# Accumulator halves over three PSUM banks, first and last two units by token half

## The reference, cut to what matters

```python
h = rms_norm(x, norm_mix_pre)
proj = h @ w_in                                  # 2048 -> 15664 columns
a_qkv, b_q, b_kv, b_gate, c_q, c_k, c_v, m_gate = jnp.split(proj, IN_OFFSETS, axis=-1)
o_a = dilated_attention(...)                     # 3 groups x 8 heads, windows 128, 512, 2048
o_b = nsa_attention(...)                         # 16 heads: compressed, selected, window branches
o_c = diff_attention(...)                        # 8 heads, two softmax maps each
g = sigmoid(m_gate.reshape(bsz, seq, 3, 2048))
mixed = g[:, :, 0] * (o_a @ w_branch_a) + g[:, :, 1] * (o_b @ w_branch_b) + g[:, :, 2] * (o_c @ w_branch_c)
x = x + rms_norm(mixed @ w_out, norm_mix_post)
x = x + rms_norm(square(relu(rms_norm(x, norm_mlp_pre) @ w_up)) @ w_down, norm_mlp_post)
```

## Time and profile before

| | |
|---|---|
| median of 3 runs | 1770.3 us (1768.73 to 1770.68) |
| the profiled execution | 1770.19 us |
| its span, first to last instruction | 1768.9 us |
| mean granted TensorE clock | 0.996 |
| TensorE busy | 1722.0 us (97%) |
| VectorE busy | 951.5 us (54%) |
| ScalarE busy | 841.3 us (48%) |
| DMA | 336.77 MB, 190 GB/s |

### The profile page before, as it was taken

One profiled execution on the slowest core, in us unless ns is written; L12 is line 12 of the kernel. 1 busy time (PEld: TensorE's weight loads), 2 busy tenths in 40 slices (PEclk: granted clock), 3 DMA queues, 4 the chain that ended last, 5 costly groups with the idle time before them and its releaser, 6 DMA issues.

```text
span 1768.9 us, 23930 instructions
## 1 busy us (share of the span) xinstructions
PE 1722.0 (97%) x8155; PEld 1401.1 (79%) x8155; DVE 951.5 (54%) x1338; ACT 841.3 (48%) x1269; POOL 55.2 (3%) x103
## 2 busy tenths in 40 slices
PE   7999999999999989999999989999999999999998
PEld 6888877777777878787888768888888888888886
DVE  5544455755555544465665465555444455554555
ACT  5443445655555555344444455444443344444442
POOL 1000010000000001000000000000000000000000
PEclk9999999999999999999999999999999999999999
DMA  7666665655566767846876565665556666655553
GB/s 236 204 181 183 194 171 133 171 154 158 164 167 191 183 176 225 277 144 220 291 239 225 190 181 176 190 182 186 190 192 194 195 189 183 188 183 185 193 195 136
DMA packets 168278, 336.77 MB, mean 190 GB/s; under 512 B 11408, under 2 KB 13664, under 8 KB 167680
## 3 DMA queue, kind: packets, MB, share of 16 engines
q1 hardware_dynamic: 162512, 317.17, 58.3%
q0 software_dynamic: 5552, 18.44, 4.5%
q10 hardware_dynamic: 128, 0.03, 0.0%
HBM read 327.11 MB, written 8.49 MB: 190 GB/s over the span
## 4 chain that ended last, share of the span: by engine, by line
PE 57%; DVE 2%; DMA 1%; ACT 1%; issue 1%; SPq 0%; ACTq 0%; DVEq 0%
PE ps L507 18%; PE ps L509 18%; PE ps L508 18%; PE ps L553 1%; DVE w_lo L1325 1%; DMA raw<-in_w_in_dram 1%; DMA gate_dram<-stage 0%; ACT w_hi L933 0%; DVE mid L1975 0%; PE ps L538 0%; PE ps L536 0%; PE ps L537 0%; DVE h_lo L1851 0%; PE ps L723 0%; PE ps L755 0%
## 5 line engine op out<-in xcount | busy, mean ns | idle before, releaser
L1325 DVE TENSOR_TENSOR w_lo<-raw,w_hi 128x1024 fp32r<-128x1024 f32 x576 | 703.2, 1225 | 685.7 <-ACT w_hi L933 666.1
L933 ACT ACTIVATE w_hi<-raw 128x1024 fp32r<-128x1024 f32 x576 | 607.2, 1059 | 636.1 <-PE ps L509 614.5
L507 PE MATMUL ps<-w_hi,h_hi 128*128 128x512 f32 (+1 forms) x1600 | 635.1, 397 | 21.7 <-ACT stage L1062 11.5
L509 PE MATMUL ps<-w_hi,h_lo 128*128 128x512 f32 (+1 forms) x1600 | 623.7, 390 | 0.0
L508 PE MATMUL ps<-w_lo,h_hi 128*128 128x512 f32 (+1 forms) x1600 | 623.0, 389 | 0.0
L507 PEld LDWEIGHTS ps<-w_hi,h_hi 128*128 128x128 f32 x1600 | 302.0, 189 | 104.2 <-issue 29.9
L509 PEld LDWEIGHTS ps<-w_hi,h_lo 128*128 128x128 f32 x1600 | 301.9, 189 | 63.5
L508 PEld LDWEIGHTS ps<-w_lo,h_hi 128*128 128x128 f32 x1600 | 302.5, 189 | 58.7
L507 PE MATMUL ps<-w_hi,u_hi 128*128 128x512 f32 x496 | 193.4, 390 | 0.0
L508 PE MATMUL ps<-w_lo,u_hi 128*128 128x512 f32 x496 | 193.0, 389 | 0.0
L509 PE MATMUL ps<-w_hi,u_lo 128*128 128x512 f32 x496 | 193.0, 389 | 0.0
(11 more groups left out here) (270 smaller groups left out, 925.8 us busy)
## 6 DMA issues: line engine op xcount, KB each, us to landing
raw<-in_w_in_dram SPq DMA_DIRECT2D x240, 512.0 KB, 3.7
raw<-in_w_up_dram SPq DMA_DIRECT2D x128, 512.0 KB, 3.8
raw<-in_w_down_dram SPq DMA_DIRECT2D x128, 512.0 KB, 4.3
raw<-in_w_out_dram SPq DMA_DIRECT2D x32, 512.0 KB, 4.2
bias<-bias_table POOLq DMA_DIRECT2D x72, 128.0 KB, 3.5
raw<-in_w_branch_b_dram SPq DMA_DIRECT2D x16, 512.0 KB, 5.5
raw<-in_w_branch_c_dram SPq DMA_DIRECT2D x16, 512.0 KB, 5.1
gate_dram<-stage SPq DMA_DIRECT2D x12, 512.0 KB, 5.8
```

The source lines that it names most:

```text
L507: pe.matmul(acc, hi[:, kc + k, tok], w_hi[:, slot, k, 0:cols], start=a, stop=False)
L509: mm = pe.matmul(acc, lo[:, kc + k, tok], w_hi[:, slot, k, 0:cols], start=False, stop=b)
L933: act.activation(w_hi[:, slot, :, :], raw[:, slot, :, :], ACT.Copy).then_inc(sem("hi_ready"), 1)
L1325: dve.tensor_tensor(w_lo[:, slot, :, :], raw[:, slot, :, :], w_hi[:, slot, :, :].bitcast(F32), ALU.subtract).then_inc(sem("lo_ready"), 1)
```

## The change

The two halves of chunk c of the slots go to banks by `slot_bank(c, t)`: banks 0, 1 and 6 in turn, (2c + t) mod 3. Bank 7 alone takes the outputs of all pairs (O_BANK), the C outputs are transposed into banks 7 and 5 (C_BANKS), the compressed probabilities into banks 4 and 5. TensorE's order in a chunk changes: in slot s = 0 it does half 0 of units 0 and 1 and half 1 of unit 0, in slot s = 1 half 1 of unit 1; the same in s = 6 and 7; between them each unit has half 0 and half 1 as before. Each half waits for `lo_ready` itself. The first half of a chunk waits for the evacuation of the second half of the chunk two before, the second half for the first half of the chunk before. The late transposes of slot 33 stand in slot 34, those of the C outputs in slots 152 to 155 instead of 152, 153, 155 and 157, and two of their splits two slots or one earlier.

```diff
...
 O_SLOT = {pr.o: p for p, pr in enumerate(PAIRS)}
 EXP_SLOT = {(pr.s + 2 if pr.kind == "a" else pr.s): p for p, pr in enumerate(PAIRS)}
 SCALE_SLOT = {(pr.s + 5 if pr.kind == "a" else pr.s + 1): p for p, pr in enumerate(PAIRS)}
-STAGE_T = {12: 6, 21: 7, 30: 8, 33: 9, 42: 10, 49: 11, 57: 12, 66: 13}
+STAGE_T = {12: 6, 21: 7, 30: 8, 34: 9, 42: 10, 49: 11, 57: 12, 66: 13}
 STAGE_CHUNK = {6: 0, 7: 1, 10: 4, 11: 5, 12: 6, 13: 7}
 BLOCKS_AT = [92, 93, 97, 98, 102, 103, 107, 108]
 B0 = 150
-C_AT = [2, 3, 5, 7]
-SPLIT_AT = [2, 2, 3, 4, 6, 8, 16, 16, 17, 17]
+C_AT = [2, 3, 4, 5]
+C_BANKS = [7, 5]
+SPLIT_AT = [2, 2, 3, 4, 5, 6, 16, 16, 17, 17]
+SLOT_BANKS = [0, 1, 6]
+O_BANK = 7
+def slot_bank(c, t):
+    return SLOT_BANKS[(2 * c + t) % 3]
 def stage_steps(n):
...
         values("v_a", 0, [tiles_out(Pos(T0["v_a"] - 1), 1, "v_a", 0)])
         with pe.Fori(1, 3) as i:
             values("v_a", i)
-        def slot_free(c):
-
-            if c <= 10:
-                return [[("evac_v", V0["q_b"] + c)], [("evac_s", S0["q_b"] + c)]]
-            return [[("evac_s", S0["gate"] + 2 * (c - 10) - 1 + t)] for t in range(2)]
+        def taken(c, t):
+            if c < 10:
+                return ("evac_s", S0["q_b"] + c + 1) if t else ("evac_v", V0["q_b"] + c + 1)
+            return "evac_s", S0["gate"] + 2 * (c - 10) + 1 + t
+        def slot_half(n, t):
+            c, s = divmod(n, CH)
+            cols = B_LAST if c == 3 else W
+            pe.wait_ge(sem("lo_ready"), XS + n + 1)
+            if s == 0:
+                if c == 0:
+                    pe.wait_ge(sem(("evac_v", "evac_s")[t]), (V0, S0)[t]["q_b"])
+                elif t:
+                    name, value = taken(c - 1, 0)
+                    pe.wait_ge(sem(name), value)
+                elif c == 1:
+                    pe.wait_ge(sem("tevac_v"), 6)
+                    pe.wait_ge(sem("tevac_s"), 6)
+                else:
+                    name, value = taken(c - 2, 1)
+                    pe.wait_ge(sem(name), value)
+            acc, tok, slot = ps[:, slot_bank(c, t), 0:cols], slice(t * P, (t + 1) * P), n % RING
+            for k in range(UR):
+                kc = UR * s + k
+                pe.matmul(acc, h_hi[:, kc, tok], w_hi[:, slot, k, 0:cols], start=kc == 0, stop=False)
+                pe.matmul(acc, h_hi[:, kc, tok], w_lo[:, slot, k, 0:cols], start=False, stop=False)
+                mm = pe.matmul(acc, h_lo[:, kc, tok], w_hi[:, slot, k, 0:cols], start=False, stop=kc == KC - 1)
+            if t:
+                mm.then_inc(sem("unit_used"), 1)
+            elif s == CH - 1:
+                mm.then_inc(sem("half_done"), 1)
         def late_tiles(n):
...
         def outputs(p):
             pr = PAIRS[p]
-            bank = 6 + pr.out % 2
+            bank = O_BANK
             pe.wait_ge(sem("pt_copied1"), p + 1)
             if pr.first:
-                wait(pe, sem("o_taken"), pr.out - 1)
+                wait(pe, sem("o_taken"), pr.out)
             if pr.kind == "c":
                 pt = p_t[:, 2 * (p % 2) + 1, :]
                 pe.matmul(ps[:, bank, 0:P], pt[:, 0:P], value(p, 0, 0), start=True, stop=True)
...
             pe.wait_ge(sem("compressed"), 1)
-            pe.wait_ge(sem("pt_copied1"), NPAIR)
+            pe.wait_ge(sem("o_split_lo"), 6)
             for t in range(2):
                 for h in range(8):
                     mm = pe.matmul(ps[:, 4 + t, 2 * NCMP * h:2 * NCMP * (h + 1)], q_b[:, h, t * P:(t + 1) * P],
...
             pe.wait_ge(sem("o_split_lo"), 6)
             for n in range(8):
                 q, t = n // 2, n % 2
-                tr = pe.transpose(ps[:, 6 + n // 4, P * (n % 4):P * (n % 4) + P],
+                tr = pe.transpose(ps[:, 4 + n // 4, P * (n % 4):P * (n % 4) + P],
                                   cmp_p[:, t, 4 * q:4 * q + 4, :].rearrange("p a n -> p (a n)"), ident[:, :])
             tr.then_inc(sem("cmp_pt"), 1)
...
         def output_transposes(j):
             pe.wait_ge(sem("c_ready"), 1)
+            pe.wait_ge(sem("pt_copied1"), NPAIR)
             pe.wait_ge(sem("o_taken"), 20)
             wait(pe, sem("o_split_lo"), j + 1 if j >= 2 else 0)
             for c in range(2):
                 for t in range(2):
-                    tr = pe.transpose(ps[:, 6 + j % 2, 256 * c + P * t:256 * c + P * t + P],
+                    tr = pe.transpose(ps[:, C_BANKS[j % 2], 256 * c + P * t:256 * c + P * t + P],
                                       o_c[:, t, P * (2 * j + c):P * (2 * j + c + 1)], ident[:, :])
             tr.then_inc(sem("o_transposed"), 1)
...
         for j, n in enumerate(C_AT):
             pe_steps.setdefault(n, []).append(lambda j=j: output_transposes(j))
         for n in range(NSLOT):
-            c, s = divmod(n, CH)
-            unit(Pos(XS + n), s % RING, h_hi, h_lo, UR * s, 0, B_LAST if c == 3 else W, s == 0, s == CH - 1,
-                 slot_free(c) if s == 0 else None)
+            s = n % CH
+            if s in (0, CH - 2):
+                slot_half(n, 0)
+                slot_half(n + 1, 0)
+            elif s not in (1, CH - 1):
+                slot_half(n, 0)
+            slot_half(n, 1)
             if n in STAGE_T:
                 late_tiles(n)
             if n in T_SLOT:
...
             if c >= 8:
                 act.wait_ge(sem("pv_done"), NA)
             dst = v_c[:, 1, W * (c - 8):W * (c - 7)] if c >= 8 else stage[:, c % 2, 1, 0:cols]
-            act.activation(dst, ps[:, 1, 0:cols], ACT.Copy, scale=scale).then_inc(sem("evac_s"), 1)
+            act.activation(dst, ps[:, slot_bank(c, 1), 0:cols], ACT.Copy, scale=scale).then_inc(sem("evac_s"), 1)
         def late_out(n):
...
                 wait(act, sem("gates_stored"), 16 * c)
             else:
                 act.wait_ge(sem("unit_used"), U0["gate"] + CH * (c + 1))
-            act.activation(stage[:, 0, h, :], ps[:, h, :], ACT.Tanh, scale=rstd_half[:, h:h + 1]).then_inc(
+            act.activation(stage[:, 0, h, :], ps[:, slot_bank(c + 10, h), :], ACT.Tanh, scale=rstd_half[:, h:h + 1]).then_inc(
                 sem("evac_s"), 1)
         def pt_copy(p):
...
             pr = PAIRS[p]
             act.wait_ge(sem("pv_done"), p + 1)
-            src = ps[:, 6 + pr.out % 2, 0:256]
+            src = ps[:, O_BANK, 0:256]
             if pr.kind == "a":
                 act.wait_ge(sem("table_stored"), 16)
                 act.activation(o_at[:, pr.out, :], src, ACT.Copy).then_inc(sem("o_taken"), 1)
...
                 act.wait_ge(sem("o_taken"), pr.out)
                 for t in range(2):
-                    sq = act.activation(c_square[:, t, :], ps[:, 6 + pr.out % 2, P * t:P * t + P], ACT.Square,
+                    sq = act.activation(c_square[:, t, :], ps[:, O_BANK, P * t:P * t + P], ACT.Square,
                                         accum_out=c_ssq[:, t, h:h + 1])
                 sq.then_inc(sem("o_taken"), 1)
...
                 act.wait_ge(sem("o_transposed"), q - 1)
                 act.wait_ge(sem("hidden_rows"), 2)
                 act.wait_ge(sem("const_loaded"), 16 * 6)
-                act.activation(o_hi[:, 8 + 2 * q:10 + 2 * q, :], ps[:, 6 + q % 2, :].rearrange("p (a n) -> p a n", a=2),
+                act.activation(o_hi[:, 8 + 2 * q:10 + 2 * q, :], ps[:, C_BANKS[q % 2], :].rearrange("p (a n) -> p a n", a=2),
                                ACT.Copy, scale=c_gain[:, 0:1]).then_inc(sem("o_split_hi"), 1)
             else:
                 act.wait_ge(sem("b_ready"), q - 5)
...
             if c >= 8:
                 dve.wait_ge(sem("pv_done"), NA)
             dst = v_c[:, 0, W * (c - 8):W * (c - 7)] if c >= 8 else stage[:, c % 2, 0, 0:cols]
-            dve.tensor_scalar(dst, ps[:, 0, 0:cols], scale, None, ALU.mult).then_inc(sem("evac_v"), 1)
+            dve.tensor_scalar(dst, ps[:, slot_bank(c, 0), 0:cols], scale, None, ALU.mult).then_inc(sem("evac_v"), 1)
         def late_out(n):
...
         def cmp_third():
             dve.wait_ge(sem("cmp_pt"), 1)
-            dve.tensor_copy(cmp_pt[:, :, :].rearrange("p (b a) n -> p b (a n)", b=2), ps[:, 6:8, :]).then_inc(
+            dve.tensor_copy(cmp_pt[:, :, :].rearrange("p (b a) n -> p b (a n)", b=2), ps[:, 4:6, :]).then_inc(
                 sem("cmp_pt_copied"), 1)
         def cmp_fourth(js):
...
                                   o_hi[:, 2 * q:2 * q + 2, :].bitcast(F32), ALU.subtract).then_inc(sem("o_split_lo"), 1)
             elif q < 6:
                 dve.scalar_tensor_tensor(o_lo[:, 8 + 2 * q:10 + 2 * q, :],
-                                         ps[:, 6 + q % 2, :].rearrange("p (a n) -> p a n", a=2), c_gain[:, 0:1],
+                                         ps[:, C_BANKS[q % 2], :].rearrange("p (a n) -> p a n", a=2), c_gain[:, 0:1],
                                          o_hi[:, 8 + 2 * q:10 + 2 * q, :].bitcast(F32), ALU.mult, ALU.subtract
                                          ).then_inc(sem("o_split_lo"), 1)
             else:
```

## The result

The changed kernel takes 1747.85 us, median of 4 runs (1746.88 to 1749.53), against 1769.66 us beside it (4 runs, 1768.73 to 1770.68): a ratio of 0.9873, 95% interval 0.9858 to 0.9887. It is faster by 21.8 us; 1749.0 were predicted. The profiled span is 1746.9 us against 1768.9.

What follows compares the result with a forecast made beforehand. TensorE, busy 1722.0 of 1768.9 us, bounds the kernel; only its idle time and low clock can be won. 21.0 + 1.0 + 2.3 - 1.0 - 2.0 = 21.3 us off 1770.3 gives 1749.0 us, range 1744 to 1753 (chance 0.70).

Steps and rivals of the forecast that it cites:

- Term one: Chunk starts in the slots: all 12 waits for tanh or evacuation go, 18.1 us plus 0.24 each, 21.0 us won.
- Term two: Doubled keys' late transposes, moved one unit later: their 1.0 us wait for VectorE's copies goes, 1.0 us won.
- Term three: Low clock after the waits near 247.5 and 573 us: 2.3 of 3.3 us lost counted as won.
- the clock at slot 142: Behind the grown w_lo wait of 1.9 us: a third of a 1.6 us clock loss counted.
- The tight places: Slot 118 and w_lo of 99, with its like in gate chunks: w_lo late, 1.0 us lost, bounds 0 and 3.
- at nothing: Single output bank, earlier C transposes (upper bound 1 us), single gate stage buffer and wait before the branches: no cost.
- Slot 142: Late raw weights: w_lo of 143 waited for 1.4 us more; 2.0 us lost with the clock, bounds 1.4 and 4.
- Rival 1: Gate chunks: ScalarE's first tanh is late and half the gates' waits come back; 1756.4 us, chance 0.12.
- rival 2: Starvation at 44 places with s = 0 and 6, w_lo wanted sooner; 1809 at full cost, chance 0.03.
- rival 4: Chunk starts: banks are not the limit, late w_lo would end each wait anyway; no change, 1770, chance 0.03.
- rival 5: Tight places grow to their bounds; 1754 us, chance 0.10.
- Rival 3: Clock falls at each of 22 chunk borders, 1.6 us lost each; 1784 us, chance 0.02.

Runs made afterwards that it cites:

- e3: Against the kernel before: two banks and the old order, the rest of the change kept (single output bank, moved transposes, w_lo waits per half); 1769.79 us, ratio 0.9996.
- e1: Whole change with three banks in rotation, but every unit in the old order (half 0, then half 1); 1747.59 us, ratio 0.9871 to the kernel before.
- e10: Whole change, but the doubled keys' transposes stay at slot 33; 1749.62 us, ratio 0.9884 to the kernel before.
- e4: Whole change with three banks, but only the first two units of a chunk by halves, the last two in old order; 1743.74 us, ratio 0.9857 to before.
- e7: Whole change, with GpSimd's 8 compression weight loads paced behind the splits instead of issued at once; 1743.87 us, ratio 0.9856 to the kernel before.
- e6: Whole change, but slots 142 and 143 in the old order; 1744.83 us, ratio 0.9859 to the kernel before.
- e5: Whole change with three banks, but only the last two units of a chunk by halves; 1749.2 us, ratio 0.9893 to the kernel before.
- e8: e4 with the compression weight loads paced as in e7; 1744.7 us, ratio 0.9859 to the kernel before.
- e2: Whole change with the order by halves, but two accumulator banks as before; 1766.64 us, ratio 0.9983 to the kernel before.
- e9: e2 with the first half's evacuation and tanh moved earlier in their queues; 1762.23 us, ratio 0.9953 to the kernel before.

## Why the prediction was right

**Term one, 21.0 us for 12 waits.** All 12 are gone, and the thirteenth (0.16 us) with them. The mechanism is shown: the evacuations run as late as they did, only nobody stands at the bank. The price of 0.24 us on top of each wait's idle time is borne out by e3 against e1, 17.0 us at full clock where the waits give 16.9; the 22.2 us between their medians hold some 5 us of clock besides.

**Term two, 1.0 us.** The wait is 0.2 us instead of 1.0, so 0.8. The prediction's own sum said that: 0.8 us of cover for a wait of 1.0 leaves 0.2, but it booked the whole. e10 shows that the move was needed for more: without it the wait is 2.9 us.

**Term three, 2.3 us, and the clock at slot 142, 0.5 us.** Both low stretches near 249 and 573 us went (3.3 us), one of 1.7 us came behind the wait at 701.60, and the third of before stayed, near 762 us. Net 1.6 us, 1.8 predicted. Neither part was hit: 3.3 for 2.3, 1.7 for 0.5. The odds were read rightly as odds, not more: where the clock falls differs from kernel to kernel beyond what the waits say (below). The prediction called itself wrong if a low clock showed at more than two places; in the slots it shows at exactly two, of which it had foreseen one. (Its "second gate chunk" is the third, that of the earlier trace rows.)

**The tight places, 1.0 us.** Neither slot 118 nor slot 99 made TensorE wait. The order was dearer by nothing there; a wait of 0.5 us for the compressed probabilities (L802) was not foreseen. It belongs neither to the banks nor to the order, since e3 has it too; "at nothing" should have held it.

**Slot 142, 1.5 us of wait.** The wait for w_lo is 2.54 us instead of 0.41, so 2.1 us more, the bound for raw weights that slip further being the part that came true: ScalarE waited 5.98 us for one of them. e4 and e7 each take it away in another way, and e6 leaves 0.3 us of it.

**The sum, and luck.** The profiled execution is 22.0 us shorter, 21.3 were predicted. The measured parts are 18.1 + 0.2 of waits and 13 x 0.24 for what lies under them, 0.8 for the doubled keys, 1.6 for the clock, less 2.1 at slot 142 and 0.5 at L802 with its 0.24: 21.0 us. 1.0 us of the 22.0 stays without a place. That the total came within a microsecond is partly luck: 1.0 us too much for the tight places and 1.0 too little for term three stood against 0.6 too little for the wait and 1.2 for the clock at slot 142. The large term, the 12 waits, was no luck.

**What I had not seen.** The prediction reads as if both parts of the change were needed, the rotation for the room and the order for the second half's bank. The runs say otherwise: the rotation carries nearly all of it (1747.59 us without the order), the order at a chunk's start takes away the waits of 3.3 us that the rotation leaves but for one of 0.5 (e4), and the order at a chunk's end gives little and costs a wait for w_lo (e5, e6). Rival 1 is refuted by the waits (none for the tanh), rival 2 by one wait for w_lo in 44 places, rival 4 by e1, and rival 5 by the time and by slots 118 and 99. Rival 3, the clock falling at changes of bank, is refuted by e4 and e5, which change bank at every half and rotate three, and show full clock in every window of 2 us before 1736 us. The Trainium skill's remark on cycling through PSUM banks (TensorE: Matmul & The Clock Gate, "A second HAM failure mode: psum-queue depth-cycling") therefore finds no support here: no fall came at a change of bank without a wait or a run of short products in front. The Trainium skill's advice to rotate independent groups through different banks, so that an evacuation runs beside the next group's matmuls (Perfetto Trace Analysis, "Matmuls"), agrees with e3 against e1: 22.2 us by the medians, 17.0 at full clock.

The best version found is e4, 1743.74 us, 0.9857 of before: three banks, and only the first two units of a chunk by halves. Its interval overlaps that of the whole change; by the ratios it is 2 to 3 us faster, which is not clear of noise. Part of that is the clock: the low stretch near 760 us, 1.7 us, is in the profiles of the whole change, e6, e7 and e8 and not in those of e1, e4, e5 and e10, though the short products in front of it are the same. At full clock e4 is at 1744.0 us and the whole change at 1743.3 and 1744.8.

## What to carry to other kernels

When a busy engine waits a little at each change of accumulator, look at where the evacuation stands in its own queue: TensorE waited up to 3 us for work of 0.7 us because of what stood in front of that work, and neither finishing the half sooner (e2) nor moving the evacuation (e9) gave what one more bank gave. Do an order change where it widens the time between complete and wanted, and check on the other side what it wants sooner: here the last pair of units wanted its weights 1.4 us sooner at the one place where a DMA was late. When waits go, look for the next step that wants another engine's work which the wait had not held up (the doubled keys): it takes back what was won there unless it moves too. And before a difference of a few us is put down to a change, count the low stretches in both profiles: here they made 5 of the 22 us between e3 and e1.

## What the runs showed of the hardware

The low clock is only loosely tied to the length of a wait. It fell behind waits of 1.00, 1.85, 1.97, 2.54 and 2.91 us (e7, before, e1, after, e10), and not behind 3.02 us in before, nor behind 1.47 and 1.68 us in e5. In e3, with nearly the same waits as before, it fell near 247, 572, 655 and 729 us, and not at 781 us, where before had it. In e7 it fell near 1020 us, in a part that no change touches and where before kept 1.00; e2 and e3 have a fall at the same work, near 1046 us, and the other ten profiles have none there. Windows of e7 (columns as in the earlier trace rows):

```profile
757.00:761.00 4.00, 4.00 (x12) 3.08 (x11) 2.44 (x6) 2.02 (x3) 0.00 (x0) 0.57 0.44 133
1020.00:1024.00 4.00, 4.00 (x12) 3.13 (x11) 1.32 (x4) 0.26 (x2) 0.00 (x0) 0.57 0.77 304
```

and of before, over the stretch that answers to the second:

```profile
1040.00:1048.00 8.00, 6.44 (x30) 4.64 (x30) 7.16 (x19) 4.60 (x14) 0.53 (x1) 1.00 0.82 220
```

TensorE did the same in front of the second: four transposes of 128 columns, then a wait of 1.00 us for h_lo. In front of the first stand only short products, the same 32 in e4, where the clock stayed full. A fall cost some 1.7 us each time but once (e2 from 779 to 786 us, 3.4 us). What decides between the two outcomes stays open; a gain of 2 us in one profile can be this alone.
